# Two changes in a hybrid-mixer kernel: where the gate bias is added, and how the heads of an attention branch are turned and scored

## The reference, cut to what matters

```python
qa, ka, va, zb, xbc, dtb, qc, kc, vc, gpre = split(h @ w_in)
# branch A, per head (8 heads, 2 maps m of 64 columns each, values of 128):
sc = einsum('bqhmd,bkhmd->bhmqk', qblk, k) * 64 ** -0.5   # q and k after rope
p  = softmax(where(allowed, sc, -inf))                   # 64-token chunks
w  = p[:, :, 0] - lam_full * p[:, :, 1]
out = einsum('bhqk,bkhe->bqhe', w, v)                    # then an RMS norm
# branch B: a Mamba-2 scan; branch C: stick-breaking attention, 16 heads of 64
proj  = einsum('bsrc,rcd->bsrd', branches, w_branch)      # r = 3 branches
gates = sigmoid(gpre.reshape(b, s, 3, 1024) + gate_bias)
merged = einsum('bsrd,bsrd->bsd', gates, proj)
return merged @ w_out
```

## Time and profile before

| | |
|---|---|
| median of 3 runs | 3062.82 us (3052.89 to 3067.95) |
| profiled execution, its own time | 3056.64 us |
| its span, granted clock | 3054.9 us, 0.896 |
| TensorE matmul, weight load busy | 2753.6 us, 2331.5 us |
| VectorE, ScalarE busy | 1568.5 us, 1217.9 us |
| heads' stage, layer 0 | about 313 to 420 us |
| branch A's gate, layer 0 | from 580.7 us |
| branch C's gate, branch B's gate, layer 0 | from 655.6 us, from 725.1 us |

### The profile page before, as it was taken

One profiled execution on the slowest core, in us unless ns is written; L12 is line 12 of the kernel. 1 busy time (PEld: TensorE's weight loads), 2 busy tenths in 40 slices (PEclk: granted clock), 3 DMA queues, 4 the chain that ended last, 5 costly groups with the idle time before them and its releaser, 6 DMA issues.

```text
span 3054.9 us, 37668 instructions
## 1 busy us (share of the span) xinstructions
PE 2753.6 (90%) x13516; PEld 2331.5 (76%) x13516; DVE 1568.5 (51%) x2147; ACT 1217.9 (40%) x1742; POOL 100.7 (3%) x82
## 2 busy tenths in 40 slices
PE   7999987799999999999779998998468579999998
PEld 5888876578788888888667877888458468888887
DVE  4554653467555355466426755553445455555554
ACT  4433553544344244245446443433310234444443
POOL 0001000000100100100000001001100000000000
PEclk9998997799899799799878998998669579999999
DMA  9544431135675375354213366543200025555553
GB/s 304 187 158 134 132 118 53 65 121 166 191 227 188 127 224 188 90 169 125 84 48 110 118 200 218 188 144 93 64 0 0 0 81 187 186 187 187 189 186 103
DMA packets 339442, 423.32 MB, mean 139 GB/s; under 512 B 28096, under 2 KB 244560, under 8 KB 339200
## 3 DMA queue, kind: packets, MB, share of 16 engines
q1 hardware_dynamic: 335952, 412.45, 42.7%
q0 software_dynamic: 3264, 9.29, 1.2%
q10 hardware_dynamic: 112, 0.04, 0.0%
HBM read 420.63 MB, written 1.05 MB: 138 GB/s over the span
## 4 chain that ended last, share of the span: by engine, by line
PE 78%; issue 7%; ACT 5%; DVE 4%; SPq 3%; DVEq 1%; DMA 1%; POOL 1%; POOLq 0%; ACTq 0%; PEldq 0%; PEld 0%
PE ps L247 17%; PE ps L248 16%; PE ps L249 16%; PE ps L489 14%; PE ps L656 4%; ACT hi L230 2%; SPq L648 2%; SPq L226 1%; DMA raw<-in_ffn_w_in 1%; PE ps L480 1%; PE ps L280 1%; PE ps L1016 1%; DVE lo L234 1%; PE ps L859 1%; ACT room L892 1%
## 5 line engine op out<-in xcount | busy, mean ns | idle before, releaser
L234 DVE TENSOR_TENSOR lo<-raw,hi 128x1024 fp32r<-128x1024 f32 x737 | 897.7, 1222 | 1055.9 <-ACT hi L230 1053.2
L230 ACT CAST hi<-raw 128x1024 fp32r<-128x1024 f32 x737 | 771.0, 1048 | 1182.4 <-PE ps L249 912.8
L247 PE MATMUL ps<-hi,xT_hi 128*128 128x512 f32 (+2 forms) x1824 | 740.6, 406 | 4.9 <-issue 4.9
L248 PE MATMUL ps<-lo,xT_hi 128*128 128x512 f32 (+2 forms) x1824 | 724.5, 397 | 0.0
L249 PE MATMUL ps<-hi,xT_lo 128*128 128x512 f32 (+2 forms) x1824 | 723.0, 396 | 0.0
L247 PEld LDWEIGHTS ps<-hi,xT_hi 128*128 128x128 f32 x1824 | 360.2, 198 | 84.0 <-issue 14.9
L249 PEld LDWEIGHTS ps<-hi,xT_lo 128*128 128x128 f32 x1824 | 358.5, 197 | 74.9
L248 PEld LDWEIGHTS ps<-lo,xT_hi 128*128 128x128 f32 x1824 | 359.6, 197 | 67.8
L489 PE MATMUL ps<-hi,hidT_hi 128*128 128x512 f32 x608 | 240.6, 396 | 23.4 <-DVE hidT_lo L575 23.4
L489 PE MATMUL ps<-hi,hidT_lo 128*128 128x512 f32 x608 | 239.4, 394 | 0.0
L489 PE MATMUL ps<-lo,hidT_hi 128*128 128x512 f32 x608 | 239.3, 394 | 0.0
(11 more groups left out here) (459 smaller groups left out, 2928.1 us busy)
## 6 DMA issues: line engine op xcount, KB each, us to landing
raw<-in_w_mix_in SPq DMA_DIRECT2D x368, 256.0 KB, 2.9
raw<-in_ffn_w_in SPq DMA_DIRECT2D x352, 256.0 KB, 3.0
raw<-in_ffn_w_out SPq DMA_DIRECT2D x176, 256.0 KB, 2.8
raw<-in_w_gate SPq DMA_DIRECT2D x128, 256.0 KB, 2.7
raw<-in_w_up SPq DMA_DIRECT2D x128, 256.0 KB, 2.9
raw<-in_w_down SPq DMA_DIRECT2D x128, 256.0 KB, 2.8
room<-in_w_ada SPq DMA_DIRECT2D x24, 1024.0 KB, 11.9
raw<-in_w_branch SPq DMA_DIRECT2D x96, 256.0 KB, 3.0
```

The source lines that it names most:

```text
L230: nc.scalar.copy(hi[c.hi_slot][:, 0:c.cols], raw[c.slot][:, 0:c.cols]).then_inc(rounded, 1)
L234: nc.vector.tensor_tensor(lo[c.slot][:, 0:c.cols], raw[c.slot][:, 0:c.cols], hi[c.hi_slot][:, 0:c.cols], ALU.subtract).then_inc(split, 1)
L247: pe.matmul(out, a[0], b[0], start=start, stop=False)
L248: pe.matmul(out, a[0], b[1], start=False, stop=False)
```

## The change

The gate's bias row is loaded into all 128 partitions (a broadcast by the load). TensorE's bias matmuls are left out. VectorE evacuates the gate's banks and adds the bias in doing so (`dve_bias`, at the place where the half's last chunk is ticked, and in the stage `fourth` behind a drain), then ScalarE takes the sigmoid in place, both tokens' tiles in one instruction. A new semaphore counts the sigmoids. To have one to spare, `Modulate` in the second block uses the counter of `Modulation`.

In branch A both maps of a head are turned by one transpose of 128 x 128: map 0 comes to lie on rows 0 to 63, map 1 on rows 64 to 127. The scores of map m are made from that half of the rows and stand in bank 2+m, both tiles side by side.

```diff
-    gate_row = sb("gate_row", [1, D])
+    gate_row = sb("gate_row", [P, D])
...
         def plan_gate(self, half):
-            def bias(pe, half=half):
-                pe.wait_ge(gate_par, (self.l * 3 + self.nth + 1) * 16)
-                for t in range(TT):
-                    pe.matmul(ps[:, self.gate[half].banks[t], :], const("ones", 1), gate_row[:, half * 512:(half + 1) * 512], start=True, stop=False)
-            self.gate.append(Dense(..., xT, bias=bias, evacs=(2, 0)))
+            self.gate.append(Dense(..., xT, evacs=(0, 2)))
...
-            pool.dma_start(gate_row[:], A["gate_bias"][self.l:self.l + 1, self.r, :]).then_inc(gate_par, 16)
+            pool.dma_start(gate_row[:], A["gate_bias"][self.l:self.l + 1, self.r, :].partition_broadcast(P)).then_inc(gate_par, 16)
...
         def act(self, act, half):
+            act.wait_ge(evac_dve, self.gate[half].evac_dve)
+            nc.scalar.activation(self.gates[:, :, cols], self.gates[:, :, cols], ACT.Sigmoid).then_inc(gate_done, 1)
+
+        def dve_bias(self, dve, half):
             b = self.gate[half]
-            act.wait_ge(used, b.done)
-            if self.nth == 2:
-                act.wait_ge(half_added, self.added(half) - 2)
+            dve.wait_ge(used, b.done)
+            dve.wait_ge(gate_par, (self.l * 3 + self.nth + 1) * 16)
             for t in range(TT):
-                nc.scalar.activation(self.gates[:, t, cols], ps[:, b.banks[t], :], ACT.Sigmoid).then_inc(evac_act, 1)
+                nc.vector.tensor_tensor(self.gates[:, t, cols], ps[:, b.banks[t], :], gate_row[:, cols], ALU.add).then_inc(evac_dve, 1)
...
-            dve.wait_ge(evac_act, self.gate[half].evac_act)
+            dve.wait_ge(gate_done, self.l * 6 + self.nth * 2 + half + 1)
...
-                for m in range(2):
-                    for t in range(TT):
-                        ins = pe.transpose(ps[0:HDA, j, m * TOK + t * P:m * TOK + (t + 1) * P],
-                                           self.qkv[:, j, t, h * P + m * HDA:h * P + (m + 1) * HDA], ident)
+                for t in range(TT):
+                    ins = pe.transpose(ps[:, j, t * P:(t + 1) * P], self.qkv[:, j, t, h * P:(h + 1) * P], ident)
...
                 for m in range(2):
-                    ins = pe.matmul(ps[:, self.BANK_S + t, m * keys:(m + 1) * keys], self.qT[e][:, m, t * P:(t + 1) * P], self.kT[e][:, m, 0:keys],
+                    rows = slice(m * HDA, (m + 1) * HDA)
+                    ins = pe.matmul(ps[:, self.BANK_S + m, t * P:t * P + keys], self.qT[e][rows, t * P:(t + 1) * P], self.kT[e][rows, 0:keys],
                                     start=True, stop=True)
...
-            nc.scalar.mul(self.qT[h % 2], view_bank(self.BANK_Q, 2, TOK)[0:HDA], HDA ** -0.5).then_inc(self.qT_done, 1)
+            nc.scalar.mul(self.qT[h % 2], ps[:, self.BANK_Q, 0:TOK], HDA ** -0.5).then_inc(self.qT_done, 1)
...
-            pool.wait_ge(used, m.A.gate[1].chunks[0].used)
+            pool.wait_ge(evac_dve, m.A.gate[1].evac_dve)
             m.C.load(pool)
-            pool.wait_ge(used, m.C.gate[1].chunks[0].used)
+            pool.wait_ge(evac_dve, m.C.gate[1].evac_dve)
             m.B.load(pool)
```

More of the change, by code:

```diff
@@ L749, in build @@
     w_mix = lambda l: layer_of(A["w_mix_in"], l)
-    half_added, gate_par = sem("branch_added"), sem("gate_par")
+    half_added, gate_done, gate_par = sem("branch_added"), sem("branch_gate"), sem("gate_par")
     class Merge:
@@ L761, in plan_gate @@
         def plan_gate(self, half):
-            def bias(pe, half=half):
-                pe.wait_ge(gate_par, (self.l * 3 + self.nth + 1) * 16)
-                for t in range(TT):
-                    pe.matmul(ps[:, self.gate[half].banks[t], :], const("ones", 1), gate_row[:, half * 512:(half + 1) * 512], start=True, stop=False)
-            self.gate.append(Dense("tok", w_mix(self.l), C_G + self.r * D + half * 512, 512, xT, bias=bias, evacs=(2, 0)))
+            self.gate.append(Dense("tok", w_mix(self.l), C_G + self.r * D + half * 512, 512, xT, evacs=(0, 2)))
             return self.gate[-1]
@@ L781, in act @@
             cols = slice(half * 512, (half + 1) * 512)
+            act.wait_ge(evac_dve, self.gate[half].evac_dve)
+            nc.scalar.activation(self.gates[:, :, cols], self.gates[:, :, cols], ACT.Sigmoid).then_inc(gate_done, 1)
+        def dve_bias(self, dve, half):
+            cols = slice(half * 512, (half + 1) * 512)
             b = self.gate[half]
-            act.wait_ge(used, b.done)
-            if self.nth == 2:
-                act.wait_ge(half_added, self.added(half) - 2)
+            dve.wait_ge(used, b.done)
+            dve.wait_ge(gate_par, (self.l * 3 + self.nth + 1) * 16)
             for t in range(TT):
-                nc.scalar.activation(self.gates[:, t, cols], ps[:, b.banks[t], :], ACT.Sigmoid).then_inc(evac_act, 1)
+                nc.vector.tensor_tensor(self.gates[:, t, cols], ps[:, b.banks[t], :], gate_row[:, cols], ALU.add).then_inc(evac_dve, 1)
         def dve(self, dve, half):
@@ L808, in build @@
         qkv = view(room, 0, 3, TT, D)
-        qT, kT = ([view(room, R_BRT + 1024 * e + 512 * j, 2, TOK)[0:HDA] for e in range(2)] for j in range(2))
+        qT, kT = ([room[:, R_BRT + 1024 * e + 512 * j:R_BRT + 1024 * e + 512 * j + TOK] for e in range(2)] for j in range(2))
         sm = [room[:, R_BRT + 2048 + 768 * e:R_BRT + 2816 + 768 * e] for e in range(2)]
@@ L943, in dve_kT @@
             dve.wait_ge(self.k_turned, self.nth(h))
-            nc.vector.tensor_copy(self.kT[h % 2], view_bank(self.BANK_K, 2, TOK)[0:HDA]).then_inc(self.kT_done, 1)
+            nc.vector.tensor_copy(self.kT[h % 2], ps[:, self.BANK_K, 0:TOK]).then_inc(self.kT_done, 1)
         def dve_mask(self, dve, h):
@@ L948, in dve_mask @@
             dve.wait_ge(self.scored, self.nth(h))
-            b0, b1 = view_bank(self.BANK_S, 2, P), view_bank(self.BANK_S + 1, 2, TOK)
+            b0, b1 = (ps[:, self.BANK_S:self.BANK_S + 2, at:at + n] for at, n in ((0, P), (P, TOK)))
             V.tensor_tensor(self.s0[e], b0, bc(mask.unsqueeze(1), [P, 2, P]), ALU.add)
@@ L1679, in dve @@
                             self.A.dve(dve, self.A.branch.index(b))
-                        elif b not in self.A.gate:
+                        elif b in self.A.gate:
+                            self.A.dve_bias(dve, self.A.gate.index(b))
+                        else:
                             if b is self.xbc[0]:
@@ L1733, in dve @@
                         self.C.dve(dve, self.C.branch.index(b))
+                    elif c == 3:
+                        for m in (self.C, self.B):
+                            if b in m.gate:
+                                dve.drain()
+                                m.dve_bias(dve, m.gate.index(b))
                 if h == 0:
@@ L1952, in build @@
     class Modulate:
-        added, squared, normed = sem("mod_added"), sem("mod_squared"), sem("mod_normed")
+        added, squared, normed = Modulation.done, sem("mod_squared"), sem("mod_normed")
         h = view(room, 8192, KT, TOK)
@@ L2009, in act @@
             if self.g:
-                act.wait_ge(self.added, 1)
+                act.wait_ge(self.added, 2)
             for t in range(TT):
```

## The result

| kernel, the same chip | median us | lowest to highest | runs |
|---|---|---|---|
| before | 3057.98 | 3052.89 to 3067.95 | 4 |
| changed | 3018.11 | 3017.70 to 3021.52 | 4 |

Changed over before is 0.9868, 95% interval 0.9838 to 0.9898. The forecast was 3024 in a range of 3008 to 3043: 39 us off the median of 3062.8 that was known then, or 3017.5 for the profiled execution. The profiled execution of the changed kernel took 3017.8 us (span 3016.0, mean granted clock 0.903) against 3056.6 (span 3054.9, 0.896): 38.8 us less. A later set of runs on another chip gave 3019.47 against 3054.78.

A forecast was written before the change was run, and what follows sets the result against it. TensorE, busy 90% of the span, was taken as the bound wherever the chain ran through it. Per layer 8.5 + 1.4 + 8.1 - 1.3 + 3.0 = 19.7 us, 39 for both, so 3062.8 becomes 3024, range 3008 to 3043.

The forecast's parts named there:

- Widths: Heads' stage: four full-width transposes for eight save 0.41 us a head; scores on both row halves save 0.65.
- cycle: Heads' stage: both cuts lie on the head's cycle, so all 1.06 us a head count, 8.5 a layer.
- the copies of qT and kT were hidden behind a chunk: Heads' stage: these copies were covered by a chunk and get shorter, so they cost nothing.
- The mask, named as next late: Heads' stage: VectorE's mask won't come earlier; of its 1.04 us ahead of the exps' copy 0.39 are left.
- Half 0: nothing, as argued: Branch A, first half: removing the bias pair gains nothing; TensorE's wait until 591.76 just grows by 1.91 us.
- both terms: Branch A, second half: 1.4 us gained by an earlier VectorE bias, and 1.7 us lost to a new clock fall.
- the rest of the 3.6: Branch A, second half: TensorE alone would be 3.6 us earlier; VectorE's queue allows 1.4 of it.
- one place has no cover: Branch C, second half: VectorE's bias delays the exponents and the scan's fourth output, costing 1.3 us a layer.
- 4.7 back: Branch C: the clock falls behind its bias pairs go, returning 4.7 us a layer; net 3.0 after a new loss.
- the first rival: The clock gives nothing back, as falls stay or turn up elsewhere: 3030 us, chance 0.21.
- The rival of the heads' clock: Heads' stage: thinner TensorE work lets the clock drop, at worst about 3224 us; chance 0.02.
- The rival of a cycle set by ScalarE and VectorE: Heads' stage: these engines set the cycle, so the cut only lengthens the transposes' wait: 3041 us, chance 0.06.

The follow-up runs named there:

- e1: The kernel before with only the heads' part of the change (transposes and scores), gates as before: 3034.86 us, 0.9948 of before.
- e7: e6 with VectorE's copy of kT moved ahead of the second split: 3007.76 us, 0.9837 of before.
- e6: The changed kernel with branch A's first bias behind the convolution, branch C's second behind the exponents, sigmoids too: 3009.44 us; again 3007.72 beside the changed kernel's 3019.47.
- e3: The kernel before, bias still on TensorE in as many passes, but 128 rows deep instead of one: 3035.08 us, 0.9950 of before.
- e2: The kernel before with only the gates' part of the change, heads as before: 3037.11 us, 0.9946 of before.
- e5: The changed kernel with branch A's gate bias and sigmoid as before, bias on TensorE: 3024.07 us, 0.9894 of before.

## Why the prediction was right

**The bound.** TensorE's time was worth its length where the chain ran through TensorE and nothing where it didn't. That reading held in every stretch but branch C, where the time taken off uncovered a wait.

**Heads.** Widths (0.41 and 0.65 us) and cycle (1.06) are as forecast to the hundredth in six heads, and e1 shows that the part gives them alone. The step "the copies of qT and kT were hidden behind a chunk" failed at one head, the second, which gained 0.23 us: the scores come 0.4 us sooner after the transposes' chunk, and kT was behind two splits. The mask, named as next late, was late for one more, the sixth, which gained 0.65: the wait ahead of its transposes grew from 0.52 to 0.91. Timeline of VectorE, changed kernel:
```profile
370.42 0.68 DVE L387 COPY room<-ps 128x512 f32<-128x512 f32 x1
...
372.51 0.68 DVE L954 TENSOR_REDUCE room<-room 128x2 f32<-128x512 f32 x1
```
Timeline of ScalarE, changed kernel:
```profile
373.22 0.40 ACT L891 ACTIVATE room<-room 128x128 f32<-128x128 f32 x1 [0.29 <-DVE room L954]
```
These are the fifth head's exps, ahead of the sixth head's transposes: they wait 0.29 us for a mask that stood behind an evacuation. In all 7.24 us came of 8.5. e7, which moves the kT copy (on top of e6, whose heads give 7.24 too), gets 8.41; that this is nearly the forecast's 8.5 is chance, since its sixth head still lacks 0.4 and its second has 0.3 more than forecast.

**Branch A.** Half 0: nothing, as argued; the difference moves by -2.0 at the pair, by -1.7 over the matmuls behind it, which no fall slows any more, and by +3.7 at the wait; -0.06 is left. Half 1: both terms came out. From the half's start to L1183 the difference moves from -4.50 to -5.79 (622.33 before, 616.54 now), so 1.3 us were won where the forecast had 1.4; the fall at the end of the wait, now 2.84 us, then takes 1.5 back, where it had 1.7. What is left is +0.18, forecast +0.3. e6 shows what held back the rest of the 3.6: with the bias behind the convolution the wait is 1.6, no fall follows and 1.7 us come.

**Branches C and B.** A pair is worth 2.0 to 2.1 us rather than 1.91, for the matmul behind a pair had paid 0.2 for the switch. Branch C gave 7.77 of 8.9. The step that failed is "one place has no cover": there is a second. Timelines of the changed kernel, VectorE, then TensorE:
```profile
653.62 1.28 DVE L795 TENSOR_TENSOR merged<-merged,ps 128x512 f32<-128x512 f32 x2
```
```profile
655.05 1.07 PE L280 MATMUL ps<-consts,hidden 128*128 128x128 f32 x8 [0.97 <-DVE merged L795]
```
The same in before, VectorE, then TensorE:
```profile
657.95 1.28 DVE L795 TENSOR_TENSOR merged<-merged,ps 128x512 f32<-128x512 f32 x2
```
```profile
662.00 1.03 PE L280 MATMUL ps<-consts,hidden 128*128 128x128 f32 x8
```
In before this L795, the last evacuation of branch A, ended at 657.95 + 1.28 = 659.23 and L280 started at 662.00, 2.77 us behind it. Ahead of L280 stood the pair with its switch (2.0 us, by the table's cells) and the slow stretch behind it (1.7 us), 3.7 us that are gone, while VectorE's addition comes only 4.33 us earlier, as does all the work ahead of the pair: the 2.77 are used up and 0.97 of waiting appears. It was the time taken back, clock included, that the prediction had not followed to the next wait.

**The new wait.** 1.30 us at the fourth output, forecast 1.3, and +1.49 in the table. e6 takes it away by order alone, so it was the bias ahead of the exponents.

**The clock.** The forecast took 4.7 back and set 1.7 against it. e3 measures the first: 4.74 in branch C, 0.4 of it inside a pair, with nothing changed but the depth and the load that it needs. The loss was 1.5. This refutes the first rival. The rival of the heads' clock didn't come: 1.00 over 300 to 425. The rival of a cycle set by ScalarE and VectorE is refuted by the 11.83.

**Not foreseen.** The stick-breaking stretch, which no part edits, gave 1.4 us in layer 0 and 2.8 in layer 1, with signs that differ between kernels (+0.40, +0.89, +1.60) and between two traces of the changed kernel. Its waits and the clock's falls lie elsewhere from trace to trace; no run here isolates it, and it stays open. That the profiled executions differ by 38.8 where 39 was forecast is therefore partly luck. The mechanisms are worth 35.4 us, a tenth less than forecast; the misses are 1.3 us a layer in the heads and 1.1 in C, against 0.5 too little in B, and some 3 us came from stretches that the change doesn't touch.

## What to carry to other kernels

Take a matmul off TensorE only where the chain says that TensorE is late, and then look for the engine that inherits the work: put the inherited work behind whatever that engine does for somebody who waits (e6: 3.2 us a layer by order alone). Look at the granted clock right behind matmuls that use few rows; if it is low with the engine busy, making them deep may win as much as removing them (e3: 15.7 us by a change of three lines, e2: 13.7). Before you read a gain off one trace, compare two traces of the same kernel: here a stretch that nobody had edited moved by 2.7 us. Two maps of 64 rows that are scored from both halves of the array cost little more than half.

## What the runs showed of the hardware

- Matmuls of 512 columns on one row let the granted clock fall to its lower level while TensorE was busy throughout, behind four of the six pairs of a layer and not behind branch B's; the same on 128 rows didn't (0.62 and 0.53 against 1.00), and a pair of 128 rows was the shorter one, 1.72 + 0.23 against 1.91 + 0.43 us.
- Two halves of the rows overlap in fp32 in either order of the program: 0.86 us for a group that took 1.51 on one half. Written map by map, the matmuls still started in pairs across the maps.
- Waits of TensorE and the clock behind them: 1.3 us, no fall; 1.6 us, none in e6 and one in e5 (0.51 over 7 us); 2.84 us, a fall (0.57). The wait's length alone doesn't tell.
